# Attention: the norm of queries and keys moved from VectorE to GpSimd, key squares summed by ScalarE

## The chip, the cores and the metric

One core of a Trainium2 chip. The metric is the device time of one execution in microseconds (us); lower is better. The engines are TensorE (PE, with its weight loads as PEld), VectorE (DVE), ScalarE (ACT), GpSimd (POOL) and SyncE (SP), which here issues most DMAs. They run side by side and meet through semaphores only.

## The reference, cut to what matters

One inference step of a decoder trunk with two layers. Each layer normalises x, projects it with one weight (`w_in`), runs sliding-window attention (A) and retention (B) on parts of the projection, and projects back (`w_out`). 2048 prompt rows and 32 sample rows pass through it. The change touches the QK-norm of A:

```
def rms_norm(x, g=None):
    y = xf * lax.rsqrt(jnp.mean(xf * xf, axis=-1, keepdims=True) + EPS)
    ... y * g

qa = rotary(rms_norm(qa.reshape(N, T, A_HEADS, A_HEAD_DIM), q_norm_g), pos, A_ROT_DIM, ...)
ka = rotary(rms_norm(ka.reshape(N, T, A_KV_HEADS, A_HEAD_DIM), k_norm_g), pos, A_ROT_DIM, ...)
```

There are 8 query heads and 2 key heads of 64 columns, so a tile of 128 rows has 10 sums of 64 squares and 10 reciprocal roots per row; the rotary part takes 16 columns of each head. All of it is float32.

## The kernel before, in words

The kernel is written engine by engine: each engine has its own program in a fixed order, and `wait_ge` on a semaphore stands before what must wait. A layer has four stages, named after their weights: A (attention), B0 and B1 (two heads of retention each), O (output projection). A stage runs over 17 steps: 16 tiles of 128 prompt rows and one step with the 32 sample rows (`s.sample`), which is step 0 in A. `L` is the layer, `s` the step, `t = s - 1`, `u = s - 2`.

TensorE, stage A (`a_step`, L715): the projection of step s in three pieces, queries (512 columns, bank `PA` or `PB`), keys and values (256), gate (512), and between their parts the attention of earlier tiles: the transposes of step t's queries and keys (`a_T`, L568 and L570, which wait for `a_qk`), its scores (`a_S`, L604, wait for `qk_lo`), and the products of probabilities and values of step u (`a_PV`, L644, wait for a transposing DMA). A piece's PSUM bank is given free by VectorE through `dve_piece`.

ScalarE, per step (`a_step`, L1882): `a_tout` copies the transposes of t out (L1708, L1709), `a_q` squares the queries into `sq` (L1666), `a_phi` and `a_vhigh` make high halves, `a_kv` squares the keys (L1683) and copies the values (L1684), `a_exp` (L1727), and `a_tanh` (L1693) makes the gate's tanh into `land`, after a wait for `a_mx >= 2 * an(L, s) - 2`, that is for both halves of the mix of step u, which read that buffer. In eight steps of each layer it also makes two high halves of B0's weights (`w_high`, L1657), which wait for VectorE's low halves.

VectorE, per step (`a_step` below, L1392): the low halves of t's transposed keys and queries (`a_lo`, L989 and L991, which release the scores), `a_land_q` (scale and gain of the queries, L929, and the sum of squares per head, L933), `a_plo` of u's second half (L1022), the masked maxima of t's scores (`a_softmax`, L1060), `a_land_k` (L945, L949), and then the norm's chain of 12 links (13 instructions, `a_norm_link`, the root by an integer guess and three Newton rounds) laid between the eight mix heads of u (L1135), `a_rotate` (L971 to L983, which raises `a_qk`), the gate (L1003), `a_plo` of t's first half (L1017), and in some steps a low half of B0's weights (`w_low`, L888). Each link waits for the semaphore of the one before. Layer 0 also carries late pieces of the first normalisation (`late_h`: `p_rstd`, `p_low`), and steps 4 to 6 the row maxima of B0's weights (`w_absmax`, L871). In layer 1 the eight weight steps are a hardware loop with registers; the others are unrolled.

GpSimd issues the weight loads (L477 to L485) and reduces one column over the partitions (`share_max`, L2029) once for each weight. In `attend` it issues B0's eight loads at c = 2 and 3 as soon as the buffer is free. SyncE issues the transposing DMAs of the probabilities (`prob_T`, L2135) after `a_plo`, the stores and the other loads.

Of the kernel before, what the change touches and what calls it, by code (L numbers as in the profile page):

```python
# [35 lines left out]
EPS = 1e-6  # L36
# [26 lines left out]
RSQRT1_LINKS = 2 + 2 * NEWTON  # L63

# [133 lines left out]
def trunk(nc, x_prompt, x_sample, cache_k, cache_v, state_ret, w_in, w_out, norm_g, q_g, k_g, sinks,  # L198
          rope_ap, rope_as, rope_bp, rope_bs, mask_a, mask_s, decay, decay_s, cols, ident,
          y_p, y_s, nk_p, nv_p, nst_p, nk_s, nv_s, nst_s, mixed):  # L200
    with ExitStack() as ctx:
# [34 lines left out]
        ss, rs, rt = sb("ss", [P, 10]), sb("rs", [P, 2, 10]), sb("rt", [P, 10])  # L236
# [71 lines left out]
        w_hi, w_lo = sem("w_hi"), sem("w_lo")  # L308
        a_qk, a_tk, a_te = sem("a_qk_ready"), sem("a_transposed"), sem("a_transposes_out")
# [28 lines left out]
        ch_g, ch_sr = sem("chain_gains"), sem("chain_sample_rope")  # L338
# [489 lines left out]
        def _(v):  # L828
# [12 lines left out]
            def rsqrt_link(ch, x, y, t, i):  # L841

                ch.wait()
                if i == 0:
                    ch.put(V.tensor_scalar(y.bitcast(I32), x.bitcast(I32), 1, None, ALU.logical_shift_right))
                    V.tensor_scalar(x, x, -0.5, None, ALU.mult)
                elif i == 1:
                    ch.put(V.tensor_scalar(y.bitcast(I32), y.bitcast(I32), -1.0, MAGIC, ALU.mult, ALU.add))
                elif i % 3 == 2:
                    ch.put(V.tensor_tensor(t, y, y, ALU.mult))  # L850
                elif i % 3 == 0:
                    ch.put(V.tensor_tensor(t, t, x, ALU.mult))
                else:
                    ch.put(V.scalar_tensor_tensor(out=y, in0=t, scalar=1.5, in1=y, op0=ALU.add, op1=ALU.mult))

# [64 lines left out]
            def a_land_q(L, s):  # L920
# [10 lines left out]
                if not s.sample:  # L931
                    last.then_inc(dve_piece, 1)
                V.tensor_reduce(ss[0:r, 0:8], sq[0:r, 0:A_W].rearrange("p (h d) -> p h d", d=A_DIM),  # L933
                                AX.X, ALU.add)

            def a_land_k(L, s):

                r, b = s.rows, s.par
                ch = Chain(v, ch_an, 4 + RSQRT_LINKS, an(L, s))
# [5 lines left out]
                last = V.scalar_tensor_tensor(out=k, in0=src, scalar=cs["A"][0:r, 0:1], in1=g, op0=ALU.mult,  # L945
                                              op1=ALU.mult)
                if not s.sample:
                    last.then_inc(dve_piece, 1)
                ch.put(V.tensor_reduce(ss[0:r, 8:10], sq[0:r, A_W:A_W + KV_W].rearrange("p (h d) -> p h d", d=A_DIM),  # L949
                                       AX.X, ALU.add))  # L950
                return ch

            def a_norm_link(s, ch, i):

                r, b = s.rows, s.par
                if i == 0:
                    ch.wait()
                    ch.put(V.tensor_scalar(ss[0:r, :], ss[0:r, :], 1.0 / A_DIM, EPS, ALU.mult, ALU.add))
                else:
                    rsqrt_link(ch, ss[0:r, :], rs[0:r, b, :], rt[0:r, :], i - 1)  # L960

            def a_norm(s, ch):
                for i in range(RSQRT_LINKS + 1):
                    a_norm_link(s, ch, i)

            def a_rotate(L, s, ch):

                r, b, y = s.rows, s.par, rs[0:s.rows, s.par, :]
                ch.wait()
# [397 lines left out]
            def layer(L, last):  # L1367
# [4 lines left out]
                def a_first(s):  # L1372

                    if s.sample:
                        a_land_q(L, s)
                        ch = a_land_k(L, s)
                        gate("A", L, s, 2, A_W, A_W + 2 * KV_W)
                        a_norm(s, ch)
# [7 lines left out]
                    ch = a_land_k(L, s)  # L1386
                    a_norm(s, ch)
                    a_rotate(L, s, ch)
                    a_softmax(L, s - 1, 1)
# [987 lines left out]
```

## Time and profile before

| | |
|---|---|
| time, median of 3 runs | 1932.44 us (1929.9 to 1935.01) |
| the profiled execution's span, first to last instruction | 1923.8 us |
| its time beside the span | the page gives the span alone; the runs are 6.1 to 11.2 us longer |
| instructions | 35859 |
| TensorE busy | 1790.1 us (93%) |
| VectorE busy | 1385.0 us (72%) |
| ScalarE busy | 721.9 us (38%) |
| GpSimd busy | 68.5 us (4%), 108 instructions |
| mean granted clock of TensorE | 0.984 |

Busy time is the union of an engine's instructions; waits and DMA issues of SyncE are not in it. A row of the timeline is one instruction or a few merged ones, with start and length; what stands in brackets is the engine's idle time before it and what ended it. A window row gives each engine's busy time in one stretch.

### The profile page before, as it was taken

What the parts mean: (1) busy time and instruction counts of PE and PEld (TensorE: products, weight loads), DVE (VectorE), ACT (ScalarE), POOL (GpSimd) and SP (SyncE); (2) the same over time, 40 slices, a digit from 0 to 9 for tenths busy, and PEclk for the clock granted to TensorE, in tenths of its full rate; (3) what the DMA queues carried; (4) which work ended last, traced back from release to release, by engine and by line L of the source; (5) the groups of instructions that cost most, each with busy time, mean ns of one, the idle gap of its engine ahead of it and who ended that gap; (6) DMA issues with size and microseconds to landing.
All of it is one profiled execution on the core that took longest, in us unless ns stands there. A gap on an engine that the chain in (4) does not pass through costs nothing.

```text
span 1923.8 us, 35859 instructions
## 1 busy us (share of the span) xinstructions
PE 1790.1 (93%) x11752; PEld 989.6 (51%) x11752; DVE 1385.0 (72%) x4744; ACT 721.9 (38%) x1841; POOL 68.5 (4%) x108
## 2 busy tenths in 40 slices
PE   0778899999999999978998999999999999999999
PEld 0345555655555555533444655555555555555444
DVE  4769999977665766678885899998766576667442
ACT  2556576631232222232443556664123222222010
POOL 3010000010000000021001000000100000000000
PEclk9899999999999999989999999999999999999999
DMA  5874545463002100089994333335400021004875
GB/s 151 205 188 72 99 94 109 82 155 118 11 11 102 64 9 11 16 211 248 248 238 133 57 77 73 72 79 107 141 12 11 28 93 54 11 11 129 199 203 157
DMA packets 353806, 196.66 MB, mean 102 GB/s; under 512 B 296624, under 2 KB 327536, under 8 KB 353552
## 3 DMA queue, kind: packets, MB, share of 16 engines
q1 hardware_dynamic: 343984, 159.89, 35.5%
q0 software_dynamic: 9728, 35.66, 5.7%
q8 instruction: 42, 0.69, 0.1%
q14 instruction: 52, 0.43, 0.1%
HBM read 88.75 MB, written 41.16 MB: 68 GB/s over the span
## 4 chain that ended last, share of the span: by engine, by line
PE 58%; DVE 22%; DMA 6%; ACT 4%; issue 4%; SPq 2%; DVEq 0%; ACTq 0%; POOL 0%
PE PB L514 23%; PE PA L514 23%; DVE r L1060 2%; DMA r<-r 2%; DVE r L1017 2%; PE S L668 2%; PE OB L687 2%; PE TK L657 2%; PE S L703 1%; DVE mix L1135 1%; PE OB L694 1%; DVE r L1022 1%; DVE w_mx L871 1%; DMA out<-r 1%; ACT w_a L1727 1%
## 5 line engine op out<-in xcount | busy, mean ns | idle before, releaser
L514 PE MATMUL PB<-w_a,hT 128*128 128x512 f16 (+1 forms) x1920 | 404.4, 361 | 0.0
L514 PE MATMUL PA<-w_a,hT 128*128 128x512 f16 (+1 forms) x1920 | 403.0, 360 | 1.0 <-DVE land L1003 1.0
L514 PEld LDWEIGHTS PB<-w_a,hT 128*128 (+1 forms) x1920 | 185.7, 99 | 178.5 <-issue 11.8
L514 PEld LDWEIGHTS PA<-w_a,hT 128*128 (+1 forms) x1920 | 186.1, 99 | 171.4 <-issue 3.8
L514 PE MATMUL PA<-w_b,r 128*128 128x512 f16 x768 | 172.9, 382 | 20.4 <-DMA r<-r 15.3
L1799 ACT ACTIVATE r<-OB 128x128 f32<-128x128 f32 (+1 forms) x136 | 36.3, 272 | 390.7 <-PE S L703 364.2
L514 PE MATMUL PA<-w_b,hT 128*128 128x512 f16 x768 | 179.6, 384 | 0.0
L514 PE MATMUL PB<-w_b,hT 128*128 128x512 f16 x768 | 176.3, 379 | 0.6 <-DVE r L1162 0.6
L514 PE MATMUL PB<-w_b,r 128*128 128x512 f16 x768 | 171.3, 379 | 0.9 <-DVE r L1284 0.9
L1182 DVE TENSOR_TENSOR r<-S,t_dec 128x256 f32<-128x256 f32 x64 | 27.2, 425 | 156.1 <-PE S L668 155.9
L514 PEld LDWEIGHTS PA<-w_b,r 128*128 128x128 f16 x768 | 74.5, 98 | 115.0 <-DMA r<-r 20.5
L1727 ACT ACTIVATE r<-r,nm,unqk 128x256 f32<-128x256 f32 x192 | 112.6, 588 | 41.2 <-DVE sd L1073 41.2
L514 PEld LDWEIGHTS PB<-w_b,r 128*128 128x128 f16 x768 | 74.9, 98 | 91.2 <-DVE r L1284 2.2
L514 PEld LDWEIGHTS PA<-w_b,hT 128*128 (+1 forms) x768 | 75.4, 99 | 85.9 <-issue 6.4
L514 PEld LDWEIGHTS PB<-w_b,hT 128*128 (+1 forms) x768 | 74.8, 98 | 77.7 <-DVE r L1162 0.9
L1811 ACT ACTIVATE r<-r,minv 128x1024 f16<-128x1024 f32 (+1 forms) x34 | 39.1, 1149 | 142.2 <-DVE minv L1245 135.7
L1213 DVE SCALAR_TENSOR_TENSOR r<-r,S 128x128 f32<-128x128 f32 x120 | 29.1, 284 | 62.6 <-PE S L703 62.4
L540 PE MATMUL PA<-w_a,hT 128*32 128x256 f16 (+1 forms) x336 | 22.4, 345 | 54.4 <-DVE w_a L888 53.5
L1792 ACT ACTIVATE r<-TK 128x512 f32<-128x512 f32 x64 | 38.2, 596 | 77.6 <-PE TK L657 77.5
L1284 DVE SCALAR_TENSOR_TENSOR r<-PB,mdd,r 128x512 f32<-128x512 f32 x32 | 23.9, 748 | 56.7 <-PE PB L514 56.2
L1259 DVE SCALAR_TENSOR_TENSOR r<-r,minv 128x1024 f16<-128x1024 f32 (+1 forms) x34 | 43.5, 1278 | 16.5 <-ACT r L1811 16.4
L1657 ACT ACTIVATE w_b<-w_b,w_gs (+1 forms) x64 | 46.1, 720 | 16.1 <-DVE w_b L888 16.1
(258 smaller groups left out, 2894.3 us busy)
## 6 DMA issues: line engine op xcount, KB each, us to landing
out<-r SPq DMA_DIRECT2D x40, 512.0 KB, 4.7
r<-mixed SPq DMA_DIRECT2D x32, 512.0 KB, 4.1
w_b<-in_w_in POOLq DMA_DIRECT2D x16, 512.0 KB, 8.8
mixed<-mix SPq DMA_DIRECT2D x32, 256.0 KB, 2.0
mixed<-mix SPq DMA_DIRECT2D x64, 128.0 KB, 1.8
w_a<-in_w_in POOLq DMA_DIRECT2D x16, 512.0 KB, 8.0
w_b<-in_w_out POOLq DMA_DIRECT2D x16, 512.0 KB, 7.1
r<-in_x_prompt SPq DMA_DIRECT2D x16, 512.0 KB, 4.6
```

What stands on the lines that cost most here:

```text
L514: last = nc.tensor.matmul(out[0:s.rows, 0:n], lhs, w16(ph, k, p, wpart), start=(k == 0 and part == 0 and wpart == 0), stop=(k == KT - 1 an ...
L657: last = nc.tensor.transpose(TK[:, i * r:(i + 1) * r], land[0:r, b, i * P:(i + 1) * P], eye[0:r, 0:r])
L668: last = nc.tensor.matmul(S0[0:r, h * r:(h + 1) * r], qkT[:, (2 + h) * r:(3 + h) * r], qkT[:, h * r:(h + 1) * r], start=True, stop=True)
L687: nc.tensor.matmul(OB[0:r, h * P:(h + 1) * P], stm[0:r, h * r:(h + 1) * r], v, start=True, stop=s.first)
L1017: V.scalar_tensor_tensor(out=ph16[0][:, 1, :], in0=r1[:, 1536:2560], scalar=P_TOP, in1=ph16[0][:, 0, :], op0=ALU.mult, op1=ALU.subtract).t ...
L1060: return V.tensor_tensor_reduce(out=prob_q[g][h // 2][:, h % 2 * 256:h % 2 * 256 + 256], in0=(SS, XX)[g][h // 2][:, (h % 2) * 256:(h % 2) ...
L1259: V.scalar_tensor_tensor(out=m[0:r, 1, :], in0=mxt[0:r, b, :], scalar=minv[0:r, b:b + 1], in1=m[0:r, 0, :], op0=ALU.mult, op1=ALU.subtract ...
L1657: A.activation(w16(kind, k, c, 0), raw(L, kind, k, c), ACT.Copy, scale=w_gs[:, run(k, 1)]).then_inc(w_hi, 1)
L1727: A.activation(x, x, ACT.Exp, scale=unqk[:, 0:1], bias=nm[:, g, h:h + 1], accum_out=rsum[:, g, h:h + 1])
L1792: last = A.activation(qkT[:, :], TK[:, :], ACT.Copy)
L1799: last = A.activation(osq[0:r, h * P:(h + 1) * P], OB[0:r, h * P:(h + 1) * P], ACT.Square, accum_out=oss[0:r, h:h + 1])
L1811: A.activation(mh_of(s)[0:r, 0, :], mxt[0:r, b, :], ACT.Copy, scale=minv[0:r, b:b + 1]).then_inc(o_hi, 1)
```

## The change

GpSimd gets `norm_qk`, called once for each step of `attend`, ahead of what stood there. It adds the query squares in halves, 64 columns of each head to 32, 16, 8, 4, 2 and 1, takes the keys' two sums from ScalarE, and computes the ten reciprocal roots. ScalarE squares the two key heads in two instructions with `accum_out`. ScalarE's `a_q` waits until the norm of the step before has ended, since it writes `sq`. VectorE keeps `a_land_q`, `a_land_k` (without sums) and `a_rotate`, which waits for GpSimd's last link; its order is also changed: in a full step the first mix half, a weight half, the rotation, the second mix half, the gate; in step 1 the rotation comes after the second softmax.

```
+HALVINGS = 6
+NORM_LINKS = HALVINGS + 3 + 4 * NEWTON
...
 def a_rotate(L, s):
-                ch.wait()
+                ch = Chain(v, ch_ar, 2, an(L, s))
+                if s.sample:
+                    v.wait_ge(a_sl, L + 1)
+                else:
+                    v.wait_ge(dve_piece, piece("A", L, s, 1) + 2)
+                v.wait_ge(ch_an, NORM_LINKS * (an(L, s) + 1))
...
 def a_step(s, k=None):
-                    ch = a_land_k(L, s)
+                    a_land_k(L, s)
                     if not u.sample:
-                        a_mix_open(L, u, 0, m0)
-                        a_mix_head(u, 0, 0)
-                        a_norm_link(s, ch, 0)
...
-                        a_norm_link(s, ch, 11)
-                        a_rotate(L, s, ch)
+                        a_mix(L, u, 0, m0)
                         if k is not None:
                             w_low(L, "B0", k, 0)
+                        a_rotate(L, s)
+                        a_mix(L, u, 1, m1)
                         gate("A", L, s, 2, A_W, A_W + 2 * KV_W)
                         a_plo(L, t, 0)
...
 def a_q(L, s):
-                if s.first:
-                    act.wait_ge(a_qk, L * STEPS + 1)
+                if not (s.fixed and L == 0 and s.c == 0):
+                    act.wait_ge(ch_an, NORM_LINKS * an(L, s))
...
 def a_kv(L, s):
-                A.activation(sq[0:r, A_W:A_W + KV_W], src[0:r, 0:KV_W], ACT.Square, scale=c[0:r, 0:1])
+                for g in range(A_KV):
+                    d = slice(g * A_DIM, (g + 1) * A_DIM)
+                    A.activation(sq[0:r, A_W:A_W + KV_W][:, d], src[0:r, d], ACT.Square, scale=c[0:r, 0:1],
+                                 accum_out=ss[0:r, A_HEADS + g:A_HEADS + g + 1])
...
+            def norm_qk(L, s):
+                r, links = s.rows, NORM_LINKS * an(L, s)
+                x, y, t = ss[0:r, :], rs[0:r, s.par, :], nt[0:r, :]
+                q = sq[0:r, 0:A_W].rearrange("p (h d) -> p h d", d=A_DIM)
+                pool.wait_ge(act_piece, apiece("A", L, s, 0) + 1)
+                for i in range(HALVINGS):
+                    if i > 0:
+                        pool.wait_ge(ch_an, links + i)
+                    d = A_DIM >> i + 1
+                    out = q[:, :, 0:d] if d > 1 else x[:, 0:A_HEADS].unsqueeze(2)
+                    G.tensor_tensor(out, q[:, :, 0:d], q[:, :, d:2 * d], ALU.add).then_inc(ch_an, 1)
+                pool.wait_ge(act_piece, apiece("A", L, s, 1) + 1)
+                pool.wait_ge(ch_an, links + HALVINGS)
+                G.tensor_scalar(x, x, 1.0 / A_DIM, EPS, ALU.mult, ALU.add).then_inc(ch_an, 1)
+                pool.wait_ge(ch_an, links + HALVINGS + 1)
+                G.tensor_scalar(y.bitcast(I32), x.bitcast(I32), -0.5, MAGIC, ALU.mult, ALU.add).then_inc(ch_an, 1)
+                pool.wait_ge(ch_an, links + HALVINGS + 2)
+                G.tensor_scalar(x, x, -0.5, None, ALU.mult).then_inc(ch_an, 1)
+                for i in range(NEWTON):
+                    n = links + HALVINGS + 3 + 4 * i
+                    pool.wait_ge(ch_an, n)
+                    G.tensor_tensor(t, y, y, ALU.mult).then_inc(ch_an, 1)
+                    pool.wait_ge(ch_an, n + 1)
+                    G.tensor_tensor(t, t, x, ALU.mult).then_inc(ch_an, 1)
+                    pool.wait_ge(ch_an, n + 2)
+                    G.tensor_scalar(t, t, 1.5, None, ALU.add).then_inc(ch_an, 1)
+                    pool.wait_ge(ch_an, n + 3)
+                    G.tensor_tensor(y, t, y, ALU.mult).then_inc(ch_an, 1)
...
             def attend(L):
                 for c in range(STEPS):
+                    norm_qk(L, Step(c))
                     if c == 2 and L == 0:
```

## Rows read from the trace of the kernel before

**Rows 1.** The page, part 1: each engine's busy us, share of the span, instructions.

```profile
PE 1790.1 (93%) x11752; PEld 989.6 (51%) x11752; DVE 1385.0 (72%) x4744; ACT 721.9 (38%) x1841; POOL 68.5 (4%) x108
```

**Rows 2.** Windows, attention steps: stretch, length, busy us by engine, clock, DMA share, GB/s.

```profile
1123.03:1141.45 18.42, 16.68 (x150) 9.97 (x149) 18.04 (x67) 10.19 (x28) 0.00 (x0) 1.00 0.35 73
...
1177.38:1194.70 17.32, 16.86 (x149) 9.87 (x150) 16.31 (x66) 11.52 (x30) 0.00 (x0) 1.00 0.36 76
...
167.73:191.07 23.34, 18.73 (x151) 11.09 (x149) 20.48 (x81) 12.81 (x32) 0.00 (x0) 0.85 0.45 80
...
191.07:211.81 20.74, 18.14 (x150) 10.76 (x149) 19.36 (x68) 11.21 (x29) 0.00 (x0) 0.92 0.47 89
...
250.09:267.90 17.81, 16.69 (x151) 9.95 (x149) 17.27 (x67) 12.61 (x32) 0.00 (x0) 1.00 0.51 103
...
339.00:355.52 16.52, 16.52 (x150) 9.96 (x149) 15.98 (x66) 11.52 (x30) 0.00 (x0) 1.00 0.43 80
```

**Rows 3.** Timeline of a layer 1 step: start us, us, engine, line, operation, names.

```profile
1163.60 0.28 PE L604 MATMUL S<-kT_hi,r 64*128 64x256 f16 x2
...
1166.88 0.36 ACT L1684 ACTIVATE land<-PB,cs_A 128x128 f32<-128x128 f32 x1
...
1175.14 0.83 DVE L971 TENSOR_TENSOR land<-land,rs 128x640 f32<-128x640 f32 x1
...
1176.46 0.67 ACT L1693 ACTIVATE land<-PA,cs_A 128x512 f32<-128x512 f32 x1
...
1176.88 0.23 DVE L983 TENSOR_TENSOR land<-r 128x80 f32<-128x80 f32 x1
...
1177.16 0.69 DVE L1003 SCALAR_TENSOR_TENSOR land<-land,PA 128x512 f32<-128x512 f32 x1
...
1177.77 1.22 DVE L1017 SCALAR_TENSOR_TENSOR r<-r 128x1024 f16<-128x1024 f32 x1
...
1178.90 0.74 DVE L888 SCALAR_TENSOR_TENSOR w_b<-w_b,w_gs  x1
...
1180.70 0.28 PE L604 MATMUL S<-kT_hi,r 64*128 64x256 f16 x2
```

**Rows 4.** Lines, whole span: count | busy us, mean ns | idle before.

```profile
L933 DVE TENSOR_REDUCE ss<-r 128x8 f32<-128x512 f32 (+1 forms) x34 | 22.9, 674 | 0.0
...
L871 DVE TENSOR_REDUCE w_mx<-w_b 128x1 f32<-128x1024 f32 x32 | 37.1, 1209 | 0.0
...
L1135 DVE SCALAR_TENSOR_TENSOR mix<-TK,rr,land 128x64 f32<-128x64 f32 x128 | 34.1, 278 | 15.6 <-PE TK L644 15.2 <-issue 0.3
...
L1799 ACT ACTIVATION_READ_ACCUMULATOR r<-OB 128x1 f32 (+1 forms) x136 | 27.0, 199 | 0.0
```

**Rows 5.** Short instructions: timeline at share_max, and lines of GpSimd and VectorE.

```profile
1145.61 0.16 DVE L882 TENSOR_REDUCE w_m<-w_mx 128x1 f32<-128x8 f32 x1
...
1145.98 0.35 POOL L2029 PARTITION_ALL_REDUCE w_am<-w_m  x1 [124.93 <-DVE w_m L882]
...
L2364 POOL MEMSET const-float32-1.0<- 128x1 f32 x1 | 0.1, 98 | 0.0
...
L837 DVE TENSOR_TENSOR ot<-oy 128x2 f32<-128x2 f32 (+1 forms) x204 | 32.7, 160 | 7.1
```

**Rows 6.** Timeline: starts of the stage in layer 0, the B0 loads of layer 1.

```profile
64.96 0.68 ACT L1666 ACTIVATE r<-PA,cs_A 32x512 f32<-32x512 f32 x1 [3.89 <-PE PA L540]
...
70.64 0.81 DVE L971 TENSOR_TENSOR land<-land,rs 32x640 f32<-32x640 f32 x1
...
79.92 2.42 PE L595 MATMUL S<-r 64*128 64x512 f32 x4 [2.85 <-ACT r L1715]
...
115.15 0.36 ACT L1684 ACTIVATE land<-PB,cs_A 128x128 f32<-128x128 f32 x1
...
118.58 0.82 DVE L971 TENSOR_TENSOR land<-land,rs 128x640 f32<-128x640 f32 x1
...
1015.09 5.96 POOL L485 DMA_DIRECT2D w_b<-in_w_in  x8 [103.94 <-DVE r L1284]
```

More of the change, by code:

```diff
@@ L234, in trunk @@
         cs = {k: sb(f"cs_{k}", [P, 8]) for k in ("A", "B0", "B1", "O")}
-        ss, rs, rt = sb("ss", [P, 10]), sb("rs", [P, 2, 10]), sb("rt", [P, 10])
+        ss, rs, rt = sb("ss", [P, 10]), sb("rs", [P, 2, 10]), sb("rt", [P, 1])
+        nt = sb("nt", [P, 10])
         mr, nm, sd, es, rsum, rr = (sb(n, [P, 2, A_GROUP]) for n in ("mr", "nm", "sd", "es", "rsum", "rr"))
@@ L308, in trunk @@
         w_hi, w_lo = sem("w_hi"), sem("w_lo")
+        a_sl = sem("a_sample_key_rows")
         a_qk, a_tk, a_te = sem("a_qk_ready"), sem("a_transposed"), sem("a_transposes_out")
@@ L337, in trunk @@
         ch_l, ch_asp = sem("chain_layer"), sem("chain_a_softmax_prompt")
[L338 removed]
+        ch_g, ch_sr, ch_ar = sem("chain_gains"), sem("chain_sample_rope"), sem("chain_a_rotate")
         BLOCKS = ("A", "B0", "B1", "O")
@@ L839, in rsqrt @@
                     ch(V.scalar_tensor_tensor(out=y, in0=t, scalar=1.5, in1=y, op0=ALU.add, op1=ALU.mult))
-            def rsqrt_link(ch, x, y, t, i):
-                ch.wait()
[L844 to L854, printed above, removed]
             def rsqrt1(ch, x, y, t):
@@ L944, in a_land_k, with a_rotate @@
                 g = qk_g[0:r, 1, :].unsqueeze(1).broadcast_to([r, A_KV, A_DIM])
[L945 to L958, printed above, removed]
-                else:
[L960 to L969, printed above, removed]
+                V.scalar_tensor_tensor(out=k, in0=src, scalar=cs["A"][0:r, 0:1], in1=g, op0=ALU.mult,
+                                       op1=ALU.mult).then_inc(a_sl if s.sample else dve_piece, 1)
+            def a_rotate(L, s):
+                r, b, y = s.rows, s.par, rs[0:s.rows, s.par, :]
+                ch = Chain(v, ch_ar, 2, an(L, s))
+                if s.sample:
+                    v.wait_ge(a_sl, L + 1)
+                else:
+                    v.wait_ge(dve_piece, piece("A", L, s, 1) + 2)
+                v.wait_ge(ch_an, NORM_LINKS * (an(L, s) + 1))
                 x = land[0:r, b, 0:A_W + KV_W].rearrange("p (h d) -> p h d", d=A_DIM)
@@ L1385, in a_first @@
                     V.memset(v16[:, 0, :, :], 0.0)
-                    ch = a_land_k(L, s)
-                    a_norm(s, ch)
-                    a_rotate(L, s, ch)
+                    a_land_k(L, s)
                     a_softmax(L, s - 1, 1)
+                    a_rotate(L, s)
                     gate("A", L, s, 2, A_W, A_W + 2 * KV_W)
@@ L1449, in a_step @@
                     else:
-                        a_norm(s, ch)
-                        a_rotate(L, s, ch)
+                        a_rotate(L, s)
                         a_mix(L, u, 1, old)
```

26 lines of the change are left out of this document (2 added, 24 removed).

## The prediction

> **What bounds the kernel now.** I read the page's busy line first [rows 1]: TensorE is busy 93% of the span, VectorE 72%, GpSimd 4%. That mean hides the stages. Only the attention stage holds changed work (about 62 to 390 us in layer 0, 1020 to 1315 us in layer 1), so I then cut that stage into its steps, from one transpose of keys (L568) to the next, and read the windows [rows 2]. In each of them VectorE is busy nearly to the end: 16.31 of 17.32 us where a step also carries two weight halves (L888), 18.04 of 18.42 us where it carries three row maxima (L871), 17.27 of 17.81 and 15.98 of 16.52 us in layer 0. TensorE's own work is 16.5 to 16.9 us a step; what it idles beside that is all that a lighter VectorE can return: 0.46 us in each of the eight steps like the window at 1177.38, 1.7 us in each of two with three maxima, 4.6 us in the window at 167.73, 2.6 us in each of two like that at 191.07, 1.1 us in five steps like the one at 250.09, and none at 339.00. The granted clock is 0.85 and 0.92 in two of them, so not all of their length is a wait. Altogether some 22 us, or 1.1% of the run, and the starts of the stage apart.
>
> Last I followed one step in the timeline [rows 3]: the scores of a step start at 1163.60 (L604), the ACT copy that ends the key piece ends at 1167.24 (L1684), VectorE starts the rotation at 1175.14 (L971) and ends it at 1177.11, the gate follows the tanh of ACT at 1177.16, the low half of the probabilities at 1177.77, a weight half at 1178.90, and the next scores start at 1180.70.
>
> **What the change takes from VectorE.** One reduction over 512 columns (0.67 us each by 22.9 us for 34) [rows 4], one over 128, and thirteen short links. In the step of [rows 3] they stood between mix heads, so I count what their going frees: about 0.6 us before the softmaxes and 1.5 us before the rotation, together 2.1 us a step. If GpSimd delivered at once, every step would fall to TensorE's own 16.5 to 16.9 us.
>
> **What it adds.** ACT squares the keys in two instructions that also sum, where it had one; the accumulator reads are 0.2 us each by L1799's [rows 4]. I take 0.4 us later for the end of the key piece, between 0.2 us (one read) and 0.8 us (two reads and a second square as long as the 0.36 us copy [rows 3]). GpSimd does six halvings of 8 x 64 squares (504 columns in all), and after the key piece 15 links on 10 columns: the mean, two that open the root, and three times four. Each waits for the one before, and the rotation waits for the last.
>
> No row shows such a link on GpSimd. From below: VectorE's link is 0.16 us and 0.035 us of idle (7.1 us over 204), 0.195 us [rows 5]. From GpSimd's own rows: it starts 0.21 us after VectorE's result (1145.77 to 1145.98), of which about 0.05 us is a separate semaphore instruction that the new links lack, and its instruction lasts 0.10 us if it only writes one column (MEMSET) and 0.35 us where all partitions exchange theirs: links from 0.26 to 0.56 us. I take 0.16 us to start and 0.20 us to read, compute and write, 0.36 us: nearer the memset, since nothing is exchanged. So 15 links are 5.4 us (2.9 to 8.4). The halvings: 6 x 0.36 us, and 504 columns at VectorE's 1.3 ns (0.67 us for 512 columns) or up to twice that, 2.8 to 3.5 us. They may run from the query squares, which end before the scores begin, to the end of the key piece, 3.64 + 0.4 us after that, and are hidden in a full step, not in the sample's.
>
> The Trainium skill, "GPSIMD Engine Reference", section "Elementwise — side-by-side cycle accounting", gives a two-input add over 2048 columns as 4497 ns on GpSimd and 2293 ns on VectorE. By it the columns of the halvings would be an estimated 1.1 us and the 15 links almost only their fixed part, which it does not give; the sum stays as it is.
>
> **The new loop.** In the old order the norm stood between the mix heads and both halves were mixed before the rotation. In the new one the rotation precedes the second half, and behind the waiting rotation stand on VectorE mix 1, the gate, a_plo and a weight half. ACT's tanh waits for mix 1 (a_mx at L1691), the gate for the tanh, TensorE's second piece of the next step for the gate, and its scores for a_lo behind all of them. Laid end to end, from scores to scores [rows 3, 4, 5]: 3.64 us to the key piece, 0.4 for the second square, 5.4 for the links, 0.1 to wake VectorE, 0.4 for one link colliding with the weight half, 1.97 rotation, 1.0 mix 1 (four of 0.27), 0.8 tanh with its wakes, 0.61 gate, 1.13 a_plo, 1.80 weight half and a_lo to the scores: 17.25 us. Before: 17.32 us [rows 2]. So the link that I hold likeliest is the one at which a weight step breaks even; the 2.1 us are freed in front of a wait.
>
> By kind of step, with 0.3 us off where VectorE's steps are not in a loop with registers:
> - eight weight steps of layer 1: 17.25 against 17.32, -0.5 us in all.
> - three maxima: 17.25 less the weight half and its collision (1.1) less 0.3, plus 3 x 1.16 (L871), 19.4 against 18.42 in two steps [rows 2, 4], and one step with two maxima taken alike. Layer 1: +3.0 us.
> - layer 0's five late-normalisation steps (1.3 us more, 17.81 less 16.52): 18.2 against 17.81, +2.0; two plain weight steps, 16.95 against 16.52, +0.8; its maxima steps, 20.7 against 20.74 (two), and 21.9 against 23.34 (two maxima, late normalisation and twelve root links of 0.195), -1.4. Together +1.3 us.
> Steady part: +3.8 us.
>
> **Starts of the stage.** The sample step hides nothing: halvings and links in a row, 3.0 + 5.4 = 8.4 us after the query squares (which end at 65.64) where VectorE rotated at 70.64, 5.0 us after them, so its rotation is late by about 3.5 us in layer 0, ahead of p_rstd and of ACT, and the scores at 79.92 for which TensorE already waits 2.85 us [rows 6] are late by as much; in layer 1 by 2.0 us, part of it under a transposing DMA. In step 2 of layer 0 the rotation at 118.58 [rows 6] follows the key piece, which ends at 115.51, by 3.07 us; now 5.4 us of links and the later key square, with wakes +2.6 us, on the path through mix, gate and prob_T. In step 3 the rotation no longer stands behind the late mix 1: -1.0 us. Together +7.1 us.
>
> **Queues moved past.** GpSimd's eight B0 loads left at once in layer 1 (1015.09, beside the output stage) [rows 6]. Now four of them stand behind norm_qk(2) and four behind norm_qk(3), about 1070 and 1088 us, beside the DMA transposes of probabilities. Their deadline, the maxima, holds; the transposes may be late. I charge 2 us (0 to 6). Each batch holds GpSimd 3 us, between norms. share_max stands before norm_qk(7), 0.6 us, covered. ACT's new wait in a_q is for a norm that ended before the rotation of the step before: nothing.
>
> **Sum.** 3.8 + 7.1 + 2 = +13 us, against the profiled execution's span of 1923.8 us. What lies around the span is 6.1 to 11.2 us by the runs (1929.9 to 1935.01); nothing of it changes, so I add the 13 to the median: 1932.4 + 13 = **1946 us**.
>
> **Rivals.**
> - *A quick link* (0.25 us). The loop is 15.6 us, TensorE's work bounds: -3.7 us in layer 1's weight steps, -1.9 in its maxima steps, -5.6 and -5.9 in layer 0, +1 at the starts, +2 loads: -14, 1918 us. For it: the memset of 0.10 us. Against: it neither reads nor waits. It decides below 0.30 us, where the result passes -4 us.
> - *Washed out*: links of 0.30 to 0.33 us, gain in the steps spent at the starts: 1928 to 1937, say 1932 us.
> - *A slow link* (0.45 us). Each 0.01 us of link is 0.15 us in some 19 steps and 0.6 us at the starts, 3.4 us: +13 + 31, 1976 us; at the upper bound 0.56, +81, 2014 us. For it: the 0.35 us of the only GpSimd row that reads.
> - *The shared port.* No row of before has VectorE and GpSimd in SBUF together. If a VectorE instruction with two SBUF inputs waited for the GpSimd instruction in flight and the reverse, the two L1022 halves, L1009 and L888 would each meet a halving or link: 0.3 us times four, half of it on the path, 0.6 us in 28 steps, +17 on top of the 13: 1963 us. The Trainium skill, "SBUF — State Buffer", section "Who interferes with whom", states such a lock for VectorE instructions with two SBUF inputs against GpSimd ones that read; by that rule this is what happens, and no run here shows it yet.
>
> **Chances.** Forecast with its neighbourhood (1939 to 1955) 0.28, quick link 0.22, washed out 0.20, slow link 0.17, shared port 0.13. A change of 0.3% (6 us) is about what a measurement of this kernel can tell from none. Faster 0.22, within 0.20, slower 0.58. Range 1918 to 1985: from the quick link to a link of some 0.47 us; the forecast's own is 1939 to 1955.
>
> **What would show it.** GpSimd start-to-start on the 10-column links: 0.36 us, else the rival. VectorE idle before L971 with GpSimd as releaser, 1 to 2 us a step. Weight steps of layer 1 at 17.2 us, steps with three maxima near 19.5. ACT waiting in tanh for mix. B0 loads of layer 1 near 1070 and 1090. The forecast is wrong if VectorE doesn't idle before the rotation, or if the step grows though the links are short.

## The result, and the profile after

The changed kernel takes **1957.16 us** (median of 4 runs, 1950.47 to 1963.48) against 1931.47 us before (4 runs): ratio 1.0133, 95% interval 1.0101 to 1.0165, 25.7 us slower. The forecast was 1946 us, slower; the sign and the range (1918 to 1985) hold, the size is half of what was measured, and the reasons given for it are for the greater part not those that the runs show. So the sign is largely luck; the section on why it was right says how. The profiled execution took 1960.16 us, its span is 1958.3 us, so 1.9 us lie around it. The same 1.7 to 1.9 us lie around the span in every run with a span on record, so the 6.1 to 11.2 us that stand for it ahead of the prediction are not that: the profiled execution of before (span 1923.8 us) was quicker than the timed ones, while this one lies in the upper half of its runs. The spans differ by 34.5 us, the medians by 25.7, so a few us of what follows are the difference between two single executions.

The page's busy line after, to be read against [rows 1]:

```profile
PE 1796.4 (92%) x11752; PEld 995.5 (51%) x11752; DVE 1317.8 (67%) x4234; ACT 736.2 (38%) x1943; POOL 281.4 (14%) x822
```

VectorE lost 67 us and TensorE does the same 11752 products; the span grew all the same. Cut by stage, from TensorE's first product with one weight to that with the next, the attention stage grew from 338.5 to 357.4 us in layer 0 and from 296.8 to 307.3 us in layer 1. Layer 0's output stage grew from 194.4 to 199.6 us, and every other stage stayed within 1.8 us. So I cut the attention stages into the steps of [rows 2]. Windows of the kernel after, same columns:

```profile
1234.28:1250.74 16.46, 16.46 (x150) 9.97 (x149) 14.49 (x51) 11.86 (x33) 6.53 (x21) 1.00 0.37 77
...
1250.74:1267.28 16.54, 16.54 (x151) 9.94 (x149) 14.82 (x52) 11.87 (x33) 6.42 (x21) 1.00 0.39 82
...
289.40:306.46 17.06, 16.52 (x150) 10.02 (x149) 15.25 (x52) 13.01 (x35) 7.06 (x21) 1.00 0.56 108
...
1153.13:1171.38 18.25, 16.51 (x150) 10.04 (x149) 16.09 (x52) 10.63 (x31) 5.42 (x21) 1.00 0.34 73
...
1171.38:1199.48 28.10, 16.68 (x150) 9.90 (x148) 15.07 (x52) 9.95 (x30) 5.82 (x22) 0.87 0.20 37
...
224.15:252.78 28.63, 19.46 (x150) 11.33 (x148) 16.34 (x53) 9.83 (x30) 5.82 (x22) 0.84 0.30 55
...
125.55:162.29 36.74, 18.35 (x151) 10.68 (x150) 15.89 (x57) 17.21 (x43) 9.24 (x26) 0.81 0.91 214
```

The first two rows answer the 17.32 us of [rows 2]: TensorE now idles nowhere in them, so these steps gained 0.8 us each. The third answers the 17.81 us, the fourth the 18.42 us. These three kinds are shorter; layer 0's steps with row maxima are not (23.83 and 20.86 us, were 23.34 and 20.74). Most of the loss sits in three steps, 23.7 us together: step 7 of each layer (28.10 us where it was 18.90, and 28.63 where it was 20.99) and step 3 of layer 0 (36.74, was 29.84). The starts of the stages, up to the first transposes of keys of full tiles, took 62.5 us where they had taken 56.6, and 45.0 where they had taken 40.5; step 8 of each layer grew by 2.3 and 1.3 us and step 3 of layer 1 by 2.1. The timeline of layer 1's step 7, with the idle time before an instruction and what ended it in brackets:

```profile
1175.56 0.16 DVE L871 TENSOR_REDUCE w_m<-w_mx 128x1 f32<-128x8 f32 x1
...
1182.03 0.38 POOL L1982 PARTITION_ALL_REDUCE w_am<-w_m  x1 [15.46 <-issue]
...
1189.54 2.25 POOL L2001 TENSOR_TENSOR r<-r 128x256 f32<-128x256 f32 x5 [7.13 <-issue]
...
1196.50 0.20 POOL L2018 TENSOR_TENSOR rs<-nt,rs 128x10 f32<-128x10 f32 x1
...
1196.81 0.82 DVE L944 TENSOR_TENSOR land<-land,rs 128x640 f32<-128x640 f32 x1 [12.70 <-POOL rs L2018]
...
1199.48 0.47 PE L572 MATMUL S<-eye,land 128*128 128x128 f32 x1 [9.36 <-DVE mix L1108]
```

The column of maxima was ready at 1175.72, but the reduction starts at 1182.03, 6.3 us later; before it started 0.21 us after its input [rows 5]. The next norm follows it by another 7.13 us in which GpSimd waits for nothing that the profile shows.
Step 3 of layer 0, in the timeline: GpSimd issues the second four B0 loads, SyncE a transposing DMA, and TensorE waits for that.

```profile
140.16 3.06 POOL L489 DMA_DIRECT2D w_b<-in_w_in  x4
...
141.69 9.74 SPq L2119 DMA_TRANSPOSE r<-r  x1
...
154.91 1.46 PE L648 MATMUL TK<-r 128*128 128x64 f16 x24 [15.08 <-DMA r<-r]
```

From issue to landing this transpose took 13.17 us; before, where the loads had left at 106.86 us, its like took 5.88:

```profile
136.93 4.34 SPq L2135 DMA_TRANSPOSE r<-r  x1
...
142.85 1.46 PE L644 MATMUL TK<-r 128*128 128x64 f16 x24 [5.53 <-DMA r<-r]
```

### The profile page after: what moved, and what is told of

Same layout as the page of the kernel before. It is cut to its first block, busy times and chain, and to the rows that moved or that the text cites. A ratio compares the mean times of both kernels' runs of the same rounds, so it can differ in the third digit from the quotient of the medians.

```text
span 1958.3 us, 36175 instructions
## 1 busy us (share of the span) xinstructions
PE 1796.4 (92%) x11752; PEld 995.5 (51%) x11752; DVE 1317.8 (67%) x4234; ACT 736.2 (38%) x1943; POOL 281.4 (14%) x822
## 4 chain that ended last, share of the span: by engine, by line
PE 68%; DVE 12%; DMA 5%; issue 4%; POOL 4%; ACT 3%; SPq 2%; DVEq 0%; ACTq 0%; POOLq 0%
PE PB L518 27%; PE PA L518 26%; DMA r<-r 2%; DVE w_mx L860 2%; PE S L672 2%; PE OB L691 2%; PE TK L661 1%; PE S L707 1%; PE OB L698 1%; PE S L608 1%; DVE r L990 1%; PE X L608 1%; DVE w_a L877 1%; DVE mix L1108 1%; DVE land L944 1%
## 5 line engine op out<-in xcount | busy, mean ns | idle before, releaser
L518 PE MATMUL PB<-w_a,hT 128*128 128x512 f16 (+1 forms) x1920 | 409.2, 364 | 0.0
L518 PEld LDWEIGHTS PB<-w_a,hT 128*128 (+1 forms) x1920 | 186.7, 99 | 181.8 <-issue 17.7
L518 PE MATMUL PA<-w_b,r 128*128 128x512 f16 x768 | 175.5, 386 | 23.9 <-DMA r<-r 14.6
L2001 POOL TENSOR_TENSOR r<-r 128x128 f32<-128x128 f32 (+7 forms) x170 | 87.3, 513 | 414.2 <-ACT r L1616 389.6
L944 DVE TENSOR_TENSOR land<-land,rs 128x640 f32<-128x640 f32 (+1 forms) x34 | 28.0, 824 | 58.7 <-POOL rs L2018 57.7
```

Source lines behind the costliest of these rows:

```text
L518: last = nc.tensor.matmul(out[0:s.rows, 0:n], lhs, w16(ph, k, p, wpart), start=(k == 0 and part == 0 and wpart == 0), stop=(k == KT - 1 an ...
L944: ch(V.tensor_tensor(x, x, y.unsqueeze(2).broadcast_to([r, A_HEADS + A_KV, A_DIM]), ALU.mult))
L2001: G.tensor_tensor(out, q[:, :, 0:d], q[:, :, d:2 * d], ALU.add).then_inc(ch_an, 1)
```

## The experiments

All were timed beside the kernel before. Ratios are to it, with 95% intervals; its medians were 1930.98 us beside runs 1 to 4, 1932.21 beside 5 to 8 and 1932.24 beside 9 to 12, so that medians of different groups compare to about 1 us. The changed kernel's own 1957.2 us is the median of four runs with an interval of some 3 us on either side, and every difference from it carries that. In the table, time is the median, the two lengths are those of the attention stages in the profiled execution, and the clock is the mean granted clock over the timed runs.

| | time, us | layer 0 | layer 1 | clock |
|---|---|---|---|---|
| before | 1931 to 1932 | 338.5 | 296.8 | 0.982 |
| after | 1957.2 | 357.4 | 307.3 | 0.974 |
| 1, reduction behind norm 7 | 1950.5 | 355.9 | 298.3 | 0.977 |
| 2, no reduction | 1943.1 | 347.5 | 298.0 | 0.976 |
| 3, loads where they were | 1968.0 | 358.6 | 312.2 | 0.972 |
| 4, edits 1 and 3 | 1953.7 | 350.8 | 306.9 | 0.974 |
| 5, loads behind norm 1 | 1952.7 | 354.7 | 307.5 | 0.975 |
| 6, maximum by DMA | 1945.4 | 353.1 | 297.3 | 0.976 |
| 7, sample's norm on VectorE | 1959.4 | 357.9 | 310.4 | 0.974 |
| 8, edits 5, 6 and 7 | 1931.6 | 339.2 | 296.1 | 0.982 |
| 9, as 8, gate first | 1932.6 | 343.3 | 295.6 | 0.980 |
| 10, as 9, four links more | 1968.4 | 367.2 | 305.8 | 0.975 |
| 11, edits 5 and 6 | 1932.8 | 342.9 | 293.4 | 0.979 |
| 12, as 9, four links fewer | 1918.0 | 334.7 | 290.2 | 0.982 |

**1. The reduction behind norm 7.**

```
-                    if c == 6:
+                    if c == 7:
                         share_max(L, "B0")
```

> The changed kernel with one edit: the reduction of B0's weight maxima over the partitions stands behind norm_qk(7) on GpSimd instead of ahead of it. In the changed kernel the reduction starts 6.3 us after its input is ready and the next norm 7.1 us after the reduction, and VectorE waits 12.7 us (layer 1) and 11.9 us (layer 0) before the rotation of step 7. Theory (GpSimd changes between two sets of its instructions around the reduction, some 6 us each way, and the norm is caught behind it): the 12 us waits of step 7 go; the reduction no longer waits for its input, so its change begins some 8 us earlier in the step, and step 8's norm, due about 17 us later, is met by 13 us of change: a wait of 0 to 4 us in step 8. Gain 12 to 18 us against the changed kernel, about 1942 us. Rival 1 (the cost is in the links of every step): no more than 2 us are gained, 1955 to 1957 us. Rival 2 (the reduction itself waits for something else, for example the weight halves of ScalarE): the same 12 us wait stands in step 8 and the time is within 3 us of the changed kernel's.

Measured: 1950.45 us, ratio 1.0096 (1.0071 to 1.0122). GpSimd in its step 7 and 8 of layer 1:

```profile
1181.88 0.20 POOL L2018 TENSOR_TENSOR rs<-nt,rs 128x10 f32<-128x10 f32 x1
1187.89 0.38 POOL L1982 PARTITION_ALL_REDUCE w_am<-w_m  x1 [5.80 <-issue]
1195.28 1.64 POOL L2001 TENSOR_TENSOR r<-r 128x256 f32<-128x256 f32 x3 [7.02 <-ACT land L1637]
```

The two changes moved with the reduction: 5.80 and 7.02 us with nothing queued ahead of them. The waits of step 7 fell from 12.7 and 11.9 us to 2.7 and 3.4; step 8 now waits 3.4 and 4.1 us. The gain is 6.7 us, half of what I expected or less; in the profiled executions 5.2 us of the rest went in layer 0's steps 9 to 13, 90.5 us long instead of 85.3 (more below).

**2. No reduction for B0.** The reduction becomes a copy:

```
+                if kind == "B0":
+                    G.tensor_scalar(w_am[:, :], w_m1[:, :], 1.0, None, ALU.mult).then_inc(w_all, 1)
+                    return
```

> The changed kernel, with B0's reduction over the partitions replaced by a GpSimd tensor_scalar that copies the one column (leaves out the maximum over the partitions in B0's scale, in both layers). Nothing else moves. Theory (change of instruction set): no reconfiguration event in the attention stage, the 12.7 and 11.9 us waits before the rotation of step 7 fall to the 0.1 to 0.8 us of their neighbours, step 7 falls from 28.1 to about 19 us in layer 1 and from 28.6 to 21 us in layer 0, and the steps after them lose their stretch at half clock: 17 to 20 us less than the changed kernel, about 1938 us. The reductions of B1 and O still pay, off the path. Rival (links in every step): 1955 to 1957 us.

This kernel leaves out the maximum over the partitions and serves for its time alone. Measured: 1943.08 us, ratio 1.0055 (1.0036 to 1.0075). Step 7 is 20.20 us in layer 1 and 22.60 in layer 0, the rotation waits 2.6 and 3.4 us there, and the attention stages are 347.5 and 298.0 us long, 9.8 and 9.3 us less than in the changed kernel. 14 us of the 25.7 are this one instruction (17 to 20 expected).

**3 and 4. The loads where they were, alone and with edit 1.**

```
+                    if c == 0 and L > 0:
+                        pool.wait_ge(dve_piece, L * PIECES + PIECE0["A"] + 1)
+                        load_weights(G, "B0", L)
                     norm_qk(L, Step(c))
                     if c == 2 and L == 0:
...
-                    if c == 2:
                         pool.wait_ge(dve_piece, L * PIECES + PIECE0["A"] + 1)
-                    if c in (2, 3):
-                        load_weights(G, "B0", L, range(4 * c - 8, 4 * c - 4))
+                        load_weights(G, "B0", L)
```

> The changed kernel with B0's weight loads put back where they ran before: in layer 1 all eight before norm_qk(0), in layer 0 all eight right behind norm_qk(2) instead of four there and four behind norm_qk(3). Theory (moved loads cost because they lie beside the transposing DMAs of the probabilities): layer 1's step 3 falls from 18.6 to 16.5 us (-2 us); in layer 0 the eight start at about 122 us and not at 107, still beside the transpose of step 3 (13.2 us in the changed kernel, 5.9 before), so that it gains 0 to 5 us. Together 2 to 7 us less than the changed kernel, 1950 to 1955 us. Rival (step 3 is long because of the norm's links): step 3 stays at 36.7 us and 18.6 us, 1957 us.

> The edits of the last-but-two and the last kernel together: reduction behind norm_qk(7), loads put back. Theory (two independent costs): the gains add, 14 to 24 us less than the changed kernel, 1933 to 1943 us, which leaves the longer starts of the stage (about 8 us) against the steady gain (about 10 us): the same time as the kernel before within 0.5%. Rival (links): 1955 us.

Measured: 1967.99 us, ratio 1.0189 (1.0166 to 1.0213), and 1953.71 us, 1.0118 (1.0094 to 1.0142). The first is 11 us slower than the changed kernel, where I expected a gain of 2 to 7; the second is 3.5 us faster, where I expected 14 to 24. In run 3 step 3 of layer 1 did fall (18.6 to 17.6 us), but GpSimd's timeline at the start of that layer shows what I had overlooked:

```profile
1041.41 5.96 POOL L489 DMA_DIRECT2D w_b<-in_w_in  x8 [104.29 <-DVE r L1257]
1056.99 1.23 POOL L2001 TENSOR_TENSOR r<-r 32x256 f32<-32x256 f32 x2 [9.62 <-issue]
```

In the changed kernel the set is changed back at 934.38, right behind A's reduction and far from any norm, and the sample's norm starts at 1044.69. Here the eight issues stand between reduction and norm, the change comes only behind them at 1047.44, and the norm starts at 1056.99. The stage's start grew from 45.0 to 51.2 us; in run 4, where the norm starts 11.5 us behind the change, it grew to 53.2 us, TensorE waits 15.60 us in it (4.09 in the changed kernel), and that eats what the moved reduction gave. Run 5 shows that eight issues alone do not cost this: with no reduction ahead of them the next sum starts directly behind them (117.47 us, below). So a place meant to test the loads found the same cost a third time, and a longer one than elsewhere; why 9.6 and 11.5 us and not some 7 is not shown.

**5. The loads behind norm 1.**

```
-                    if c == 2 and L == 0:
+                    if c == 1 and L == 0:
...
-                    if c == 2:
+                    if c == 1:
                         pool.wait_ge(dve_piece, L * PIECES + PIECE0["A"] + 1)
-                    if c in (2, 3):
-                        load_weights(G, "B0", L, range(4 * c - 8, 4 * c - 4))
+                        load_weights(G, "B0", L)
```

> The changed kernel with B0's eight weight loads right behind norm_qk(1) in both layers, about 107 us and 1070 us, where GpSimd has nothing to do, and not four behind norm_qk(2) and four behind norm_qk(3). The run with the loads ahead of norm_qk(0) in layer 1 had put the change of GpSimd's instruction set behind the loads and so into the sample's norm; this place has no reduction ahead of it. Theory (the loads of the changed kernel fall beside the transposing DMAs of step 3): the two transposes before TensorE's products in step 3 of layer 0 return in about 6 us, TensorE's waits there fall from 15.4 us to some 6 us, step 3 of layer 0 from 36.7 to about 30 us, of layer 1 from 18.6 to about 16.5 us; norm_qk(2) of layer 0 starts 2 us late, +1 us in step 2. Together 6 to 9 us less than the changed kernel: 1948 to 1951 us. Rival (step 3 waits because of the norm): 1955 to 1957 us, step 3 at 36 us.

Measured: 1952.74 us, ratio 1.0103 (1.0079 to 1.0128), 4.4 us less than the changed kernel (6 to 9 expected).

```profile
111.30 6.16 POOL L489 DMA_DIRECT2D w_b<-in_w_in  x8 [23.13 <-issue]
117.47 2.30 POOL L2001 TENSOR_TENSOR r<-r 128x256 f32<-128x256 f32 x5
```

The loads leave the transpose of step 3 at 6.25 us, and step 3 of layer 0 falls from 36.7 to 29.5 us, as expected. In the profiled execution 3.7 us of that come back in steps 9 to 13 (below), and layer 1 gains nothing (307.5 us).

**6. The maximum over partitions by DMA.** Complete and exact, without the reduction:

```
+                if kind == "B0":
+                    v.wait_ge(tp_in, (L + 1) * 16)
+                    V.tensor_reduce(w_am[:, :], w_mb[:, :], AX.X, ALU.max).then_inc(w_all, 1)
...
                     if c == 6:
-                        share_max(L, "B0")
+                        pool.wait_ge(w_max, wn(L, "B0") + 1)
...
+                            G.dma_start(tops[L:L + 1, :].rearrange("o p -> p o"), w_m1[:, :]).then_inc(tp_out, 16)
+                    if c == 7:
+                        pool.wait_ge(tp_out, (L + 1) * 16)
+                        G.dma_start(w_mb[:, :], tops[L:L + 1, :].broadcast_to([P, P])).then_inc(tp_in, 16)
```

> The changed kernel with the maximum over partitions of B0's weights made without GpSimd's reduction: the column goes to DRAM by a DMA behind norm_qk(6), comes back to all partitions as a row by a DMA behind norm_qk(7), and VectorE takes the maximum of the row at the end of step 7. Complete and exact. Theory (change of instruction set): the same as the run that left the maximum out, no 12 us wait in step 7 and no stretch at half clock behind it, plus 0.2 to 1 us for the extra VectorE instruction and a late DMA: 1942 to 1946 us. Rival (that run gained because the maximum came at once, not because the set stayed): VectorE waits several us for the DMA and the time stays above 1952 us.

Measured: 1945.36 us (12 runs, 1933.71 to 1961.3), ratio 1.0060 (1.0035 to 1.0085): as run 2, and as expected. So run 2 gained because the reduction went, and not because the maximum came sooner.

**7. The sample's norm on VectorE.** In `a_first`, for the sample: the reduction, the mean and `rsqrt` on VectorE ahead of `a_rotate`, the gate behind it; `norm_qk` from step 1 on.

> The changed kernel with the norm of the sample's step (step 0 of each layer) alone back on VectorE, all other steps on GpSimd. Theory (the sample hides nothing, so halvings and 15 GpSimd links in a row stand on the path): VectorE's rotation of the sample in layer 0 comes at about 70.6 us instead of 72.3, the first transposes of keys at about 105 us instead of 108.2, and in layer 1 1 to 3 us sooner than in the changed kernel. Together 3 to 6 us less than the changed kernel: 1951 to 1954 us. Rival (the start is set by the input's DMAs and the first normalisation, not by the sample's norm): no change, 1956 to 1958 us.

Measured: 1959.35 us, ratio 1.0144 (1.0116 to 1.0172): nothing gained (3 to 6 us expected). I had also moved the gate behind the rotation, and TensorE waited for it, 2.21 us in layer 0 and 4.86 in layer 1. Its scores came 1.4 us sooner than in the changed kernel, but ran as slowly (3.78 us, 2.42 before).

**8 and 9. The edits 5, 6 and 7 together, then with the gate first.**

```
                         a_land_k(L, s)
+                        gate("A", L, s, 2, A_W, A_W + 2 * KV_W)
                         ch = Chain(v, ch_vn, 1 + RSQRT_LINKS, L)
...
                         a_rotate(L, s)
-                        gate("A", L, s, 2, A_W, A_W + 2 * KV_W)
```

> The three edits together: loads behind norm_qk(1), maximum over partitions by DMA, the sample's norm on VectorE. Theory: three independent costs taken away, 14 + 8 + 4.5 us from 1957, 1926 to 1932 us: the steady gain of some 10 us, measured on the steps of the changed kernel, less what stays of the longer first steps. If the steady gain is real this is faster than the kernel before by 0 to 0.3%. Rival (GpSimd's links also cost in every step): 1936 us or more, and the steps of the attention stage are no shorter than before.

> The kernel with three edits (loads behind norm_qk(1), maximum by DMA, sample's norm on VectorE; 1931.6 us), with the gate of the sample's step ahead of its norm, as in the kernel before, and not behind its rotation, where that kernel had it and TensorE waited 4.85 us for it in layer 1 and 1.11 us in layer 0. Theory (that wait was my own edit's cost and hid what the sample's norm on VectorE gives): the start of layer 1's stage, from its first product to the first transposes of keys, falls from 44.4 us to about 40.5 as before, layer 0's by up to 1 us: 1926 to 1929 us, faster than the kernel before by 0.2 to 0.3%. Rival (TensorE then waits for the rotation instead): 1930 to 1932 us.

Measured: 1931.64 us, ratio 0.9995 (0.9980 to 1.0011), and 1932.55 us, 1.0004 (0.9989 to 1.0019). The whole loss is gone; the gate's place is worth nothing (3 to 6 us expected), since in layer 1 TensorE waits 3.52 us for the rotation instead of 4.85 for the gate.

**11. The edits 5 and 6 alone.**

> The changed kernel with two edits, loads behind norm_qk(1) and the maximum over partitions by DMA; the sample's norm stays on GpSimd. Alone they gave 4.4 and 11.8 us of 25.5. Theory A (costs add; the sample's norm on VectorE alone gave nothing): 1957 - 16 = 1941 us. Theory B (the costs are joined by TensorE's clock, which the records show at half in 80 to 90 us where the sample's scores had waited 4 us, and which each of the three waits can bring down): the sample's part is worth several us only with the others gone, and this stands at 1936 to 1940 us, with a mean granted clock of 0.978, between the changed kernel's 0.973 and 0.982. If it measures 1932, the sample's norm costs nothing.

Measured: 1932.77 us, ratio 1.0006 (0.9989 to 1.0024). So the sample's norm is worth the same on either engine, within about 1 us, and two edits that touch none of the norm's own work take away the whole loss. They seem not to add: 11.8 and 4.4 us alone, 24.4 together. By the scatter of the four kernels' runs those 8 us more have a standard error of some 4 us, so that the two costs help each other is likely and not certain. Windows of this kernel: a late-normalisation step, step 7 and a weight step of layer 1.

```profile
309.60:326.67 17.07, 16.52 (x151) 10.03 (x150) 15.25 (x52) 13.01 (x35) 7.08 (x21) 1.00 0.56 108
1153.73:1173.88 20.15, 16.70 (x151) 9.87 (x149) 18.05 (x60) 10.63 (x31) 7.89 (x23) 1.00 0.36 69
1240.16:1256.62 16.46, 16.46 (x150) 9.96 (x149) 14.49 (x51) 11.86 (x33) 6.53 (x21) 1.00 0.37 77
```

**10 and 12. Four links more, four fewer**, on the kernel of run 9: `ROUNDS = 4` or `2` for GpSimd's Newton rounds instead of 3.

> The kernel with the gate first and one round of Newton more in GpSimd's norm alone, four more links on 10 columns (19 instead of 15). Theory (the loop of the prediction with the link as measured, 11.85 us and 0.30 us a link, bounded below by TensorE's 16.5 us): 15 links give 16.35, covered by TensorE; 19 give 17.55 us, so that layer 1's eight weight steps grow from 16.5 to 17.3 to 17.6 us (+8 us in all), layer 0's late-normalisation steps from 17.06 to about 18.1 (+5), its two plain ones by 0.7 each, the maxima steps by about 1.2 each (+6), the first steps +2: about 20 us more than its base. Rival (the chain has slack, the old waits were not for the links): under 5 us more, weight steps stay at 16.5 us.

> The kernel with the gate first and one round of Newton less in GpSimd's norm, 11 links instead of 15 (less exact roots). Theory (same loop): layer 1's weight steps stay at TensorE's 16.5 us, no gain; layer 0's late-normalisation steps fall from 17.06 to 16.5 (-2.7 us), the maxima steps by about 1 us each where the rotation waits 1.1 to 3.3 us (-5), steps 1 and 2 of each layer -1: about 8 us less than its base. Rival (the chain has slack everywhere): within 2 us.

Measured: 1968.40 us, ratio 1.0196 (1.0174 to 1.0219), 36 us more than its base (20 expected); and 1917.98 us (1912.75 to 1924.0), ratio 0.9933 (0.9910 to 0.9956), 14.6 us less (8 expected). Of all that ran, the last alone is faster than the kernel before, with roots of one round less. Windows of the kernel with four more, two weight steps and a late-normalisation step:

```profile
1271.78:1288.69 16.91, 16.60 (x150) 9.95 (x149) 14.26 (x50) 11.71 (x34) 7.99 (x25) 1.00 0.37 78
1288.69:1306.06 17.37, 16.69 (x150) 9.94 (x149) 14.18 (x50) 12.24 (x34) 7.93 (x25) 1.00 0.36 75
323.66:344.16 20.50, 18.13 (x150) 10.79 (x149) 15.70 (x51) 12.58 (x35) 9.03 (x25) 0.92 0.44 90
```

The loop model holds in layer 1's weight steps: eight of them grew by 6.0 us in all (8 expected), and the wait before the rotation from 0.10 us to 1.29, about four links of 0.30. Steps 6 and 7 grew by 4.2 us together (2.4 expected). It fails in layer 0: the five late-normalisation steps grew by 12.0 us (5 expected), three of them to some 20.5 us. In all five of them the meeting of VectorE and GpSimd that the next section describes takes place (0.68 us for a sum of 4 elements; in the base, run 9, in three), and in the last three the rotation waits 3.7 us.

## Why the prediction was right in sign and wrong in its terms

That the kernel came out slower, as forecast, is largely luck. The term that was to make it slower in the steps, the link, was too high, and what made it slower is a term that stood at nothing and one that stood at 2 us. With both put right, the change is worth nothing (run 11). The sum itself is also off by a little: 1932.4 + 13 is 1945.4 and not 1946.

- **The link.** Forecast 0.36 us. In layer 1 the 15 links start from 1162.16 to 1166.37, 14 intervals of 0.30 us, and each lasts 0.20 to 0.24 us. First and last of them, in the timeline after:

```profile
1162.16 0.20 POOL L2004 TENSOR_SCALAR ss<-ss 128x10 f32<-128x10 f32 x1 [3.68 <-ACT land L1637]
...
1166.37 0.20 POOL L2018 TENSOR_TENSOR rs<-nt,rs 128x10 f32<-128x10 f32 x1
```

  This is the term with the greatest leverage (3.4 us for each 0.01), and it was mis-sized. At 0.30 the prediction has its rival "washed out", 1928 to 1937 us, and that is what the changed kernel measures without its two accidents, the reduction between norms and the moved loads: 1932.8 us (run 11). The prediction's own sign says the same: VectorE was to idle 1 to 2 us before the rotation, and in layer 1's weight steps it waits 0.1 us.
- **The steady part.** Forecast +3.8 us. In the kernel of run 11, steps 4 to 16 take 234.7 us in layer 0 (237.2 before) and 219.4 in layer 1 (225.3): -8.4 us. The break-even of the weight steps (17.25 us) fell with the link; they run at TensorE's 16.5 us.
- **The starts.** Forecast +7.1 us, and 2 for the loads. Up to the end of step 3 the kernel of run 11, whose loads are already out of the way of step 3, spends 110.8 us (104.0 before) in layer 0 and 76.6 (74.2) in layer 1: +9.1 us, against 7.1. The cause that I named for the largest of them, the sample's norm on GpSimd, is not borne out: moved back to VectorE it gained nothing in time (runs 7, 8 and 11), and in run 8 the same stretches are 106.7 and 79.3 us, 2.7 and 5.1 us more than before.
- **"share_max stands before norm_qk(7), 0.6 us, covered."** This is the step that failed. It was priced by the reduction's own 0.35 us and by its 0.21 us of start [rows 5], on an engine that had no elementwise work before. With the norm on the same engine it stands between two changes of the instruction set, and VectorE waits 12.7 and 11.9 us before the rotation, of which 2.6 and 3.4 stay without the reduction (run 2). It costs 11.8 us when it alone goes (run 6), 20.0 us where the loads had been put right first (run 11 against run 5).
- **The loads.** Forecast 2 us (0 to 6). Measured 4.4 us alone (run 5), 12.6 us once the reduction was gone (run 11 against run 6), which is above the stated bound. The mechanism, transposes made late, was right. I looked for it in layer 1, and it cost most in layer 0: there the eight loads moved from 107 us to 122 and 140 us, where a transpose more than doubled.
- **The shared port.** As a rival I gave it 17 us. Something like it is in the traces. In two kernels that are the same in these steps (runs 6 and 11), VectorE's short sum of two inputs meets GpSimd's first halving or just precedes it. Timelines, first run 6, then run 11:

```profile
321.64 2.35 POOL L2006 TENSOR_TENSOR r<-r 128x256 f32<-128x256 f32 x5 [7.00 <-ACT r L1621]
321.78 0.68 DVE L1063 TENSOR_TENSOR rr<-rsum,es 128x4 f32<-128x4 f32 x1
```

```profile
312.33 0.15 DVE L1063 TENSOR_TENSOR rr<-rsum,es 128x4 f32<-128x4 f32 x1
312.40 3.53 POOL L2006 TENSOR_TENSOR r<-r 128x256 f32<-128x256 f32 x5 [7.21 <-ACT r L1621]
```

  Behind a halving in flight 4 elements take VectorE 0.68 us instead of 0.15, and everything of the step behind them comes later; the step is 17.80 us instead of 17.07 and hands the same meeting on to the next. In the other order GpSimd pays: five halvings take 3.53 us instead of 2.35, without harm. That the meeting makes the step long is read from the rows and not tested by an edit; in all profiles of the kernels with 15 links each step of 17.7 us or more among these five has the 0.68 us, and each shorter one 0.15 or 0.16. By profiles, layer 0's steps 9 to 13 ran in the short rhythm after and in runs 2, 3, 8 and 11 (one step excepted in 3 and 8), in the long one in runs 1, 4, 5, 6 and 7, and in run 9 they changed from short to long at step 11. That is 3.7 us in five steps, and perhaps one reason why single edits gained less than their sum; one profile of each kernel doesn't say how often its timed runs took which rhythm. The Trainium skill, "SBUF — State Buffer", section "Who interferes with whom", says that a VectorE instruction with two SBUF inputs contends with a GpSimd instruction that reads SBUF, and that the order of issue decides who waits; the rows agree. Of the instructions that the rival named, L1022's halves went from 0.68 to 0.74 us in the mean, L1009 (0.34) and L888 (0.74 to 0.75) stayed, so the 17 us were too high.
- **The clock.** I priced nothing for it. The mean granted clock fell with the waits (table). An example, in the timeline after:

```profile
81.05 3.78 PE L599 MATMUL S<-r 64*128 64x512 f32 x4 [3.98 <-ACT r L1668]
```

  The same four products took 2.42 us before [rows 6]. TensorE had paused 2.54 us at 74.28 and 3.98 us ahead of this row, and from 80 to 90 us it was granted 0.51, nearly all at 1.2 GHz, where before it had 0.83. From the means (0.9735 after, 0.982 before), the time at 1.2 GHz is (1 - 0.9735) / 0.5 of 1957 us, 104 us, against 70 us before. If TensorE worked all that time, half of the difference, 17 us, would be lost: an upper bound, since in part of it TensorE idled. A wait that is followed by a stretch at the lower clock pays twice, and this too may join the two costs. How much of the interaction it is, no run here separates.
- **Open.** Layer 0's output stage was 194.4 us before and 194.8 in run 2, and 196.5 to 202.0 us in all others. After, one wait of TensorE is 6.97 us there (2.23 before), and ahead of it ScalarE had waited 9.21 us for a DMA into `hT` (4.20 before). Run 11 has this stage at 200.3 us and layer 0's first transposes 5 us later than before, and still the time of before in the median; the profile of before was quicker than all its timed runs, so a part of both may be that one execution. No edit here was aimed at either, nor at the 3.7 us waits of run 10.

## What to carry to other kernels

- Price a move to another engine by what that engine already does. A single instruction of another kind among an engine's regular work can cost many times its own length (0.38 us here, 12 us or more of the run), and its place in the order (runs 1 and 3) decides who pays. Look for it in the trace by a gap "issue" on both sides of the odd instruction.
- When work lands on a queue that also issues DMAs, list every issue behind it with its old and its new time, in every layer, and look at what else moves data at the new one.
- Where a sum hangs on one unmeasured duration, the case at its other end deserves the same care as the forecast, and a loop that stands at its corner is to be priced from both sides: four links more cost 36 us, four fewer gave 14.6.

## What the runs showed of the hardware that I had not expected

- GpSimd between its partition reduction and its elementwise instructions: 5.6 to 6.0 us from the record MODIFY_POOL_CONFIG to the reduction, and 6.7 to 7.5 us from the reduction's end to the next sum, in the six kernels that reduce between norms (after and runs 1, 3, 4, 5 and 7). Where nothing but time stood behind it (after A's reduction, 934.38 to 1044.69) it was free. Eight DMA issues between the two kept the change from starting early (runs 3 and 4).
- A dependent GpSimd instruction on 128 x 10 elements: 0.20 to 0.27 us, 0.28 to 0.33 us from start to start, in some nineteen of twenty.
- A VectorE instruction on 4 elements with two SBUF inputs: 0.15 us, or 0.68 us behind a GpSimd sum in flight; and steps of 17.07 or 17.80 us that keep either rhythm for up to five steps.
